# Two routing stages filled with dense independent products, and three waits of the second block's row stages rearranged

## What is computed

```python
kv = mem @ w_kv                      # memory keys and values: depend on the input mem alone
...
logits = (x2d @ w_router) + router_bias          # 1024 -> 16
experts, weights = (two best of the best group)  # the routing
h = silu(xblk @ w_gate[e]) * (xblk @ w_up[e]);  y = h @ w_down[e]
x = layer_norm(DEEPNORM_ALPHA * x + f, ln2_g[l], ln2_b[l])
```

## Time and profile before

| | |
|---|---|
| median of 3 runs | 2289.58 us (2288.24 to 2292.69) |
| the profiled execution | 2292.44 us, of which the span of the profile is 2290.6 us |
| TensorE busy (modelled ends) | 2220.6 us, 97% of the span |
| VectorE, ScalarE busy | 1166.8 us, 447.9 us |
| chain that ended last, by engine | PE 79%, DMA 9%, DVE 7% |
| data moved | 452.59 MB, 198 GB/s over the span |

### The profile page before, as it was taken

One profiled execution on the slowest core, in us unless ns is written; L12 is line 12 of the kernel. 1 busy time (PEld: TensorE's weight loads), 2 busy tenths in 40 slices (PEclk: granted clock), 3 DMA queues, 4 the chain that ended last, 5 costly groups with the idle time before them and its releaser, 6 DMA issues.

```text
span 2290.6 us, 24720 instructions
## 1 busy us (share of the span) xinstructions
PE 2220.6 (97%) x9777; PEld 1396.5 (61%) x9777; DVE 1166.8 (51%) x1953; ACT 447.9 (20%) x1022; POOL 3.1 (0%) x20
## 2 busy tenths in 40 slices
PE   9999999999999999999999998999999999998998
PEld 7765445444357754445444685778888887554453
DVE  4765874211167257752111447764565432586766
ACT  1002402211121014022111316320000102352010
POOL 0000000000000000000000000000000000000000
PEclk9999999999999999999999999999999999999999
DMA  9346744799963459346999620002221225303340
GB/s 355 133 188 248 335 183 166 306 423 428 428 272 124 174 195 403 126 164 269 424 427 428 271 79 33 1 17 95 74 109 52 76 76 204 127 10 147 138 175 18
DMA packets 36431, 452.59 MB, mean 198 GB/s; under 512 B 5224, under 2 KB 7130, under 8 KB 8794
## 3 DMA queue, kind: packets, MB, share of 16 engines
q1 hardware_dynamic: 33152, 447.76, 48.2%
q10 hardware_dynamic: 3162, 3.21, 0.4%
HBM read 449.91 MB, written 1.05 MB: 197 GB/s over the span
## 4 chain that ended last, share of the span: by engine, by line
PE 79%; DMA 9%; DVE 7%; DVEq 2%; issue 1%; ACT 1%; SPq 0%; POOLq 0%; POOL 0%; ACTq 0%
PE banks L573 75%; DMA ring<-in_w_exp_up 9%; PE banks L1596 1%; PE banks L726 1%; DVE tiny L3094 1%; DVE tiny L2423 1%; DVE arena L2437 1%; DVE arena L2131 0%; DVE arena L3109 0%; DVE ring L2168 0%; DVE arena L2142 0%; DVE banks L2420 0%; ACT arena L2089 0%; DVEq L2143 0%; DVEq L2436 0%
## 5 line engine op out<-in xcount | busy, mean ns | idle before, releaser
L573 PE MATMUL banks<-ring,arena 128*64 128x512 f32 (+2 forms) x3318 | 966.1, 550 | 20.8 <-DMA ring<-in_w_exp_up 6.5
L573 PEld LDWEIGHTS banks<-ring,arena 128*128 128x128 f32 (+1 forms) x3318 | 450.8, 166 | 505.2 <-issue 469.7
L573 PE MATMUL banks<-arena 128*128 128x128 f32 (+6 forms) x1568 | 237.4, 343 | 7.8 <-issue 3.3
L573 PE MATMUL banks<-X,ring 128*128 128x256 f32 x1024 | 222.6, 379 | 0.9 <-DVE arena L2376 0.5
L573 PEld LDWEIGHTS banks<-X,ring 128*128 128x128 f32 x1024 | 194.4, 190 | 29.9 <-issue 3.3
L573 PEld LDWEIGHTS banks<-arena 128*128 128x128 f32 (+2 forms) x1568 | 153.2, 174 | 66.0 <-issue 31.3
L573 PE MATMUL banks<-arena,ring 128*128 128x256 f32 (+1 forms) x736 | 178.7, 399 | 2.4 <-ACT arena L1926 2.3
L573 PEld LDWEIGHTS banks<-arena,ring 128*128 128x128 f32 x736 | 139.0, 190 | 38.7 <-issue 16.4
L2267 DVE TENSOR_TENSOR arena<-arena,banks 128x512 f32<-128x512 f32 x16 | 11.0, 687 | 258.2 <-ACT arena L1744 258.2
L573 PE MATMUL banks<-ring 128*128 128x256 f32 x616 | 137.0, 379 | 0.0
L2168 DVE TENSOR_TENSOR ring<-ring 128x2048 f32<-128x2048 f32 (+1 forms) x56 | 119.7, 2138 | 18.0 <-ACT arena L1706 12.5
(11 more groups left out here) (356 smaller groups left out, 1899.1 us busy)
## 6 DMA issues: line engine op xcount, KB each, us to landing
ring<-in_w_in SPq DMA_DIRECT2D x37, 2048.0 KB, 12.1
ring<-in_w_exp_gate SPq DMA_DIRECT2D x32, 2048.0 KB, 13.5
ring<-in_w_exp_up SPq DMA_DIRECT2D x32, 2048.0 KB, 16.6
ring<-in_w_exp_down SPq DMA_DIRECT2D x32, 2048.0 KB, 11.9
ring<-in_w_ada SPq DMA_DIRECT2D x24, 2048.0 KB, 10.5
ring<-in_w_ffn SPq DMA_DIRECT2D x22, 2048.0 KB, 7.6
ring<-in_w_out SPq DMA_DIRECT2D x8, 2048.0 KB, 12.0
ring<-in_w_down SPq DMA_DIRECT2D x8, 1408.0 KB, 6.1
```

The lines of the kernel that those rows point to most:

```text
L573: ins = nc.tensor.matmul(out, weights, moving, start=start, stop=stop)
```

## The change

1. **l = 0 routing.** The values half of the memory projection of l = 1 is computed densely (two banks, 8 matmuls of 512 columns each) as `filler(0)`, split around the routing's small work, and `filler(1)`. Its tile is loaded ahead of the experts' tiles, so 85 tiles are loaded in l = 0. After the experts the keys are computed densely (4 chunks of 8 matmuls of 256 columns) in place of the memory unit and its key transposes; VectorE's sums for it go.
2. **l = 1 routing.** The fillers are context chunks 0 to 3 (16 matmuls of 256 columns each), copied to a spare place and later, by one ScalarE copy, into place. w_in_2's first tile is loaded for this ahead of the experts and once more behind them.
3. **Order in both.** `logits(0)` moves behind `turned_rows(xres, 1)`, the context transposes or gain rows behind the position matmuls; on ScalarE the exponential and the table load move ahead of their copies.
4. **Second model.** The first product of unit 1 moves into unit 0, ahead of its waits, in `seven_products` and in `late_tail`. `x_normed` moves earlier on VectorE: in `mix_units` ahead of one sum, in `down_units` ahead of the wait for bank 5.
5. The convolution unit of l = 1 runs in pieces of 256 columns, as l = 0's does; places, counts and slots follow.

```diff
 # SyncE
             for l in range(DEPTH):
                 if l:
-                    for c in (0, 1):
-                        tile(block_of("w_mem_kv", l * 2 + c))
+                    tile(block_of("w_mem_kv", l * 2))
...
                 for name in ("w_br_attn", "w_out"):
                     for c in (0, 1):
                         tile(block_of(name, l * 2 + c))
+                tile(a["w_in_2"][0] if l == DEPTH - 1 else block_of("w_mem_kv", (l + 1) * 2 + 1))
...
-            for c in range(3):
+            for c in (1, 2, 0):
                 tile(a["w_in_2"][c], c)
 # TensorE
+                w_fill = slot(next_tile(), DC, 512)
+
+                def filler(f, k0, k1):
+                    b = FILL_BANKS[f]
+                    if k0 == 0:
+                        free(b)
+                    if l < DEPTH - 1:
+                        for k in range(k0, k1):
+                            ins = mm(bank[b][:], memT[:, k, f * P:f * P + P], w_fill[:, k, :],
+                                     start=(k == 0), stop=(k == DC - 1))
+                    else:
+                        for i in range(2 * k0, 2 * k1):
+                            c, k = divmod(i, DC)
+                            ins = mm(bank[b][:, c * T:c * T + T], w_fill[:, k, (2 * f + c) * P:(2 * f + c) * P + P],
+                                     hctx[:, k, :], start=(k == 0), stop=(k == DC - 1))
+                    if k1 == DC:
+                        full(ins, b, "act")
                 free(4)
+                filler(0, 0, 4)
+                turned_rows(xres, 1)
                 logits(0)
-                turned_rows(xres, 1)
+                full(logits(1), 4, "dve")
                 token_rows(0)
-                full(logits(1), 4, "dve")
                 token_rows(1)
                 xtok_copied = (s_read["act"], C.value("read_act"))
-                if l == 0:
-                    pe.wait_ge(s_ctx_loaded, 16)
-                    turned_input("ctx_2", "act")
-                else:
-                    for j in range(2):
-                        gain_row(mix_diag[:, 8 * j:8 * j + 8, :], (0, 1))
+                filler(0, 4, DC)
                 pe.wait_ge(s_chosen, C.next("chosen"))
...
+                if l == 0:
+                    pe.wait_ge(s_ctx_loaded, 16)
+                    turned_input("ctx_2", "act")
+                else:
+                    for j in range(2):
+                        gain_row(mix_diag[:, 8 * j:8 * j + 8, :], (0, 1))
+                filler(1, 0, DC)
+                used()
                 pe.wait_ge(*xtok_copied)
                 more, last_scatter = expert_pairs()
...
                 if l == DEPTH - 1:
-                    pe.wait_ge(s_ctx, 1)
-                    context_chunk(0)
-                    context_chunk(2)
+                    context_chunk(4)
+                    context_chunk(6)
                     normed_rows_turned()
                 else:
-                    memory_unit(l + 1, 1 + ROWS_SUMMED * (l + 1), normed_rows_turned)
-            for n in (1, 3):
+                    w = slot(next_tile(), DC, 512)
+                    for c in range(MEM_HEADS):
+                        if c == 2:
+                            normed_rows_turned()
+                        feature_product(w, c, memT, T, "act")
+                    used()
+            for n in (5, 7):
                 context_chunk(n)
...
-            for n in range(4, 12):
+            for n in range(8, 12):
                 context_chunk(n)
+            next_tile(0)
 # TensorE, seven_products: unit 1's first product, at the end of unit 0's transposes
+                    if u == 1:
+                        w = w_next
+                    else:
+                        first_product(w)
                     if u == 0:
                         full(gate_up(1, w[:, KH:DC, 0:2 * P], ...
                         for tc in range(TC):
                             rows_turned(mix_rows[TC + tc], CTX_TURN_BANKS[tc])
+                        w_next = slot(next_tile(1), DC, 4 * P)
+                        first_product(w_next)
                     pe.wait_ge(s_wsum, C.next("wsum"))
 # TensorE, late_tail: after_second of unit 0
+                def second_unit_begun():
+                    rows_turned(row_parts(late_rows[:, 1, :]), (7, 6))
+                    s_next.extend(next_tile(late.pop(0)) for half in range(2))
+                    free(0)
+                    for k in range(KH):
+                        ins = mm(bank[0][:], rows[:, k, 0:P], slot(s_next[0], DC, 512)[:, k, :],
+                                 start=(k == 0), stop=(k == KH - 1))
+                    ins.then_inc(s_full["act"], 1)
+                    last[0] = (s_first, C.next("first"))
 # ScalarE
                 act.drain().then_inc(s_xtok, 1)
+                filler_copied(0)
+                act.wait_ge(s_logit_max, C.next("logit_max"))
+                fn(tiny[:, 34:36], tiny[:, 34:36], ACT.Exp).then_inc(s_logit_exp, 1)
+                table_of(ACT.Sigmoid)
                 if l == 0:
                     input_turned(X, T)
...
+                filler_copied(1)
                 expert_pairs()
 # VectorE, row_unit
                 if x_done:
                     drain().then_inc(s_late_rows, 1)
+                if x_normed and x_turned:
+                    x_normed()
                 filled()
                 tt(y, u_three, bank[5][:], ALU.add)
...
                 row_gained(1, 2 * u + 1, gains[1], y)
+                if x_normed and not x_turned:
+                    x_normed()
                 tt(u_two, u_two, bank[5][:], ALU.add).then_inc(s_unit_read, 1)
                 drain()
-                if x_normed:
-                    x_normed()
+                if x_turned:
+                    x_turned()
                 filled()
```

More of the change, by code:

```diff
@@ L37 @@
 X_BANKS, CTX_TURN_BANKS = ((7, 0), (3, 2)), ((7, 6), (3, 2))
+FILL_BANKS = (3, 2)
 FIRST_BANKS = (0, 1, 4, 5)
@@ L40 @@
 LOAD_PAIR = 3
-UNIT_SLOTS = [[(84 * l + i) % 6 for i in UNIT_AT[l]] for l in range(DEPTH)]
+UNIT_SLOTS = [[i if i is None else (TILES1[0] * l + i) % 6 for i in UNIT_AT[l]] for l in range(DEPTH)]
 LATE_SLOTS = [(2, 0, 1, 3, 4, 5)[i % 6] for i in range(3 + 2 + FU2 + 6)]
@@ L969, in expert_pairs @@
                 return more, last_scatter
-            in2 = []
+            in2 = [slot(c, DC, 512) for c in range(3)]
             def context_chunk(n):
                 if n % 4 == 0:
-                    in2.append(slot(next_tile(), DC, 512))
+                    next_tile(n // 4)
                 b = CTX_BANKS[n // 2]
@@ L1054, in _ @@
                 pe.wait_ge(s_conv, C.next("conv"))
-                unit(cbT, conv_sums, summed=ROWS_SUMMED * l + 2 + l, kh=CC // 2,
-                     width=512 if l else 256)
+                unit(cbT, conv_sums, summed=ROWS_SUMMED[l] + 2, kh=CC // 2, width=256)
                 if l == 0:
@@ L1365, in seven_products, with first_product @@
                     summed = (lambda: (s_tsum, C.next("tsum"))) if u == 0 else None
-                    gate_up(0, w[:, 0:KH, 0:2 * P], hx[:, 0:KH, :], row_chunk if u == 0 else None) \
-                        .then_inc(s_full["act"], 1)
-                    last[0] = (s_first, C.next("first"))
+                    def first_product(w_):
+                        gate_up(0, w_[:, 0:KH, 0:2 * P], hx[:, 0:KH, :], row_chunk if u == 0 and w_ is w else None) \
+                            .then_inc(s_full["act"], 1)
+                        last[0] = (s_first, C.next("first"))
[3 more added lines that the diff above has]
+                        first_product(w)
                     if u == 0:
@@ L1420, in tile_sums @@
                     pe.wait_ge(s_tile_sums, C.next("tile_sums", count))
-                ins = product(0, src[:, lo, first], wa[:, lo, :], lo_ready)
-                if ends:
+                if not begun:
+                    ins = product(0, src[:, lo, first], wa[:, lo, :], lo_ready)
+                if begun:
+                    pass
+                elif ends:
                     ins.then_inc(s_full["act"], 1)
@@ L1462, in late_tail @@
                 wa, wb = (slot(next_tile(late.pop(0)), DC, 512) for half in range(2))
-                late_unit(rows, late_sums, wa, wb, KH, 512, ROWS_SUMMED * DEPTH + 1, lo_ready=heads, hi_ready=other_heads)
+                late_unit(rows, late_sums, wa, wb, KH, 512, ROWS_SUMMED1 + 1, lo_ready=heads, hi_ready=other_heads)
                 used(2)
                 rows_turned(row_parts(late_rows[:, 0, :]), (7, 6))
+                s_next = []
+                def second_unit_begun():
[6 more added lines that the diff above has]
+                    ins.then_inc(s_full["act"], 1)
+                    last[0] = (s_first, C.next("first"))
                 for u, (width, c0, nc_) in enumerate(LATE_UNITS):
-                    s = next_tile(late.pop(0))
+                    s = s_next[0] if u == 1 else next_tile(late.pop(0))
```

(19 more changed lines are left out.)

79 lines of the change are left out of this document (41 added, 38 removed).

## The result

The changed kernel takes **2276.06 us** (median of 4 runs, 2275.37 to 2277.62), against 2291.14 us for the kernel before beside it (4 runs, 2288.24 to 2293.74): ratio 0.9931, 95% interval 0.9917 to 0.9946, some 15 us faster. Forecast were 2271 and a range of 2263 to 2280. The profiled execution took 2275.37 us, 17.1 less than the 2292.44 of the one before.

What follows compares the result with a forecast made beforehand. The DMA's tile loads were taken to bound the expert stages, TensorE with short waits most of the rest. Terms summed to -18.4 us: 2274.0 against the profiled 2292.44, 2271.2 against the median, given as 2271, range 2263 to 2280.

Steps and rivals of the forecast that it cites:

- The frame: Expert stages: the DMA sets the pace, so a later gather(0) moves the experts' end by as much.
- Rival (d): Experts hide the later gather(0), one tile in each layer, 9.8 us: 2261; chance 0.04.
- Routings: Last output-row sum to gather(0): the added dense products lengthen it by 12.0 us in l = 0, 10.8 in l = 1.
- with a fall some 2.5 us into the logits they end near 396.7: Routing of l = 0: the clock falls during the logits, which would end at 395.15 if it held.
- Rival (a): The clock holds in both routings, +9.0 and +7.9 us: 2265.4; chance 0.15.
- Rival (c): In both routings the clock stays low from the logits until gather(0), 11.2 us more each: 2293.6; chance 0.05.
- End of l = 0: Behind the experts, dense keys replace the memory unit, so x's first product comes 11.2 us sooner.
- keys 0 and 1 cost the same 6.9 before the transposes: End of l = 0: the first two dense key chunks take 6.87 us, like the memory unit's first 16 records.
- h2's cover: End of l = 1: with four chunks less (-13.8 us), h2's scaling is still ready 6 us before x's products.
- seven products: Second model: unit 1's first product fills the wait behind the transposes and the clock stays up, -4.7 us.
- Late tail: Second model: unit 1's first product fills a wait, -3.45, and the clock gives 1.5 (bounds 0 and 3.1): -4.9 us.
- Rival (b): VectorE becomes the bound where unit 1 lost its first product, both 3.45 us come back: 2278; chance 0.15.

Runs made afterwards that it cites:

- experiment 4: Changed kernel with seven of eight parts of filler(1) left out in both routings, so results are incomplete: 2270.59 us.
- experiment 3: Changed kernel with logits(0) ahead of filler(0)'s first half and token_rows(0) between the two logits: 2271.78 us, ratio 0.9911; repeated 2272.53, 0.9922.
- second profile: The changed kernel run once more, unaltered: 2276.18 us, ratio 0.9935 to the kernel before.
- Experiments 7 to 10: Changed kernel with four tiny products more in the routing of l = 0: 2280.94 us; twelve more: 2290.56; three filler(1) products less: 2274.42; and experiment 10.
- experiment 1: Kernel before with only the second model's part of the change: 2276.61 us, ratio 0.9937.
- experiment 10: Changed kernel with logits(0) first, filler(1) halved, convolution unit of l = 0 in 512 columns, half the l = 1 filler chunks in 128: 2268.58 us, ratio 0.9899.
- first-model kernel: Changed kernel with the second model's part undone: 2292.18 us, ratio 0.9998 to the kernel before.

## Why the prediction was right, point by point

**The frame held.** A later gather(0) moved the experts' end by as much: loads 11.6 us after it, up loads 29.4 apart, 0.3 us of 10 hidden, and in experiment 4 6.0 us at gather(0) gave 5.4 and 5.5 at the end of each layer's experts. Rival (d) is out. One reading of the prediction was wrong without harm: it says that nothing is loaded during the routing, but the earlier trace rows has a DMA share of 1.03 in 394 to 396. Two down tiles were being loaded there, until 397.6, and no further tile until 414.56. With the added tile these loads end at 400.5, and the next again comes only behind gather(0).

**Routings.** +10.5 and +9.7 for +12.0 and +10.8. The mechanism, narrow products bringing the clock down, is shown by experiment 3, where apart they do not. Mis-sized was the step "with a fall some 2.5 us into the logits they end near 396.7": the fall came behind the logits in the first profile, 4.3 us after they began, and the low clock ended before filler(0)'s second half. In the second profile, with the fall 2.7 us after they began, l = 0 took 29.03, as forecast. Rival (a), the clock holds, did not come true in the changed kernel (0.50 at 398 to 400), but its 25.9 and 26.6 us (16.90 + 9.0, 18.69 + 7.9) are nearly what the stages take with the logits apart, 25.47 and 26.46. (By the prediction's own steps, with 1.8 us for 16 transposes at the high clock, they come to some 8.7 and 7.6 more, 25.6 and 26.3.) Rival (c) is out: the clock was back at 400. The rule of the Trainium skill that rival (a) names ("TensorE: Matmul & The Clock Gate", section "HAM oscillation — how this bites in real kernels"), no long idle gaps, holds for both orders and does not tell them apart; the trace does.

**End of l = 0.** -9.8 for -11.2. The step that failed is "keys 0 and 1 cost the same 6.9 before the transposes": they took 8.35, 1.18 of it the pause. I had priced every product by its columns alone, the smaller pieces of the convolution unit too ("twice the records at half the length, 0"). The number of products ahead also sets where the borders of the code lie. In l = 0 the change put the fillers' 16 products ahead of these keys; the smaller pieces of l = 1 come behind them. Experiments 7 to 10 show that the number decides.

**End of l = 1.** -13.8 for -13.8; h2's cover held and the last loads cost nothing. Key transposes -0.5 for -0.4.

**Second model.** Down -5.8 for -5.7, mix -0.5 for -0.5, seven products -4.1 for -4.7: the third row sum came 1.5 us behind the second and not 1.1, so waits of 0.78 and 0.41 were left. (The terms given for the down units add up to 5.6, not 5.7.) Late tail -5.5 for -4.9: the first wait shrank by 3.8 (5.06 to 1.27), where 3.45 were expected, but a new wait for a tile sum took 0.97 of it back, as the step had feared; the clock stayed at 1.00, and the same 48 records took 21.1 us in place of 23.7, which is 2.6 and not the 1.5 taken. Rival (b), 2278, is out: experiment 1 keeps the gain, and no new wait for sums stands in units 1. The attention of l = 1 lost 1.7 by a fall of the clock that no step had.

**The sum.** -17.1 for -18.4 between profiled executions: the routings gave 2.6 more and the late tail 0.6, the end of l = 0 took 1.4, the seven products 0.6, the fall in the attention 1.7, and the start was 1.0 later (the second profile has 385.98, so that is no part of the change); the rest is made of differences under 0.5. That it came out within 1.3 us is in part luck: some 3.2 us of misses one way stand against 4.7 the other way. The other 3.7 us from 2271 to the median of 2276.06 are no term of the sum: the kernel before had a median of 2291.14 in this comparison and not 2289.58, and its profiled execution lay 1.3 above that, the changed kernel's 0.7 below its own.

The balance by parts differs from what the forecast's sum suggests: there the first model's share is -2.6 of -18.4, and by the granted clock that much comes and goes from kernel to kernel: measured alone it is nothing. Its worth shows only once both of its faults are mended: with the logits apart and the code shifted the kernel takes 2268.58 (0.9899), some 8 us below the second model's part alone (2276.61, 0.9937). Up to 1.7 of that may be the fall in the attention, which experiment 1 has and experiment 10 has not.

## What to carry to other kernels

Where loads set the pace behind a point, work ahead of that point costs its full length, so moving work into a stage pays only for the idle time that it fills: here 13.8 us of products made the stage 10.5 longer, and 8.6 with the better order. Spread products with few columns among dense ones, and ask of every move what the clock did with it before calling a difference of 2 or 3 us a gain. And count TensorE's instructions where code follows a conditional part while the DMA is full: look for "issue" pauses in unbroken rows of products, and shift the code by a few instructions.

## What the hardware showed that I had not expected

- The end of a piece of TensorE's code under full weight traffic: pauses of 0.77 to 5.58 us, set by the number of instructions ahead; the packet of 16 KB ended 1.35 to 1.44 us before work went on in eight profiles, and 1.6 and 1.7 us before it at the two longest pauses.
- 36 records, all 16 columns wide, in one stretch of 4.3 us (392.28 to 396.6) came ahead of a fall to 1.2 GHz with TensorE never idle in between; a fall 2.5 to 5.3 us after the first of them is in all 16 routing stages of the eight profiles with this order. The same products in two stretches, with a dense product between, left it at 2.4 GHz in four profiles, with a wait of 0.57 us behind the second.
- The price of the same wait in clock varies: at the down units' transposes the same 3.94 us cost a stretch at 0.50 that was twice as long in the first-model kernel as in the kernel before (6.8 us for 3.4). A part that should gain 3 us measured nothing by this.
